# Strassen weight sums of an up projection: accumulating transfers in place of GpSimd additions

## What is computed

```python
def swiglu(h, w1, w3, w2):
    return (jax.nn.silu(h @ w1) * (h @ w3)) @ w2
...
yp = yp + swiglu(rmsnorm(yp, norm_ffn_g[l]), ffn_w1[l], ffn_w3[l], ffn_w2[l])
```

## Time and profile before

| | us |
|---|---|
| median of three runs | 1737.89 |
| the profiled execution: span from its first to its last instruction | 1735.7 |
| its own time, the median taken for it: 2.2 us lie around the span | 1737.9 |
| TensorE busy | 1702.0 |
| VectorE busy | 1058.7 |
| ScalarE busy | 683.9 |
| GpSimd busy | 370.5 |
| feed-forward part, layer 0 | 465 to 865 |
| feed-forward part, layer 1 | 1306 to 1735.7 |

### The profile page before, as it was taken

One profiled execution on the slowest core, in us unless ns is written; L12 is line 12 of the kernel. 1 busy time (PEld: TensorE's weight loads), 2 busy tenths in 40 slices (PEclk: granted clock), 3 DMA queues, 4 the chain that ended last, 5 costly groups with the idle time before them and its releaser, 6 DMA issues.

```text
span 1735.7 us, 27688 instructions
## 1 busy us (share of the span) xinstructions
PE 1702.0 (98%) x11360; PEld 1543.0 (89%) x11360; DVE 1058.7 (61%) x1717; ACT 683.9 (39%) x1219; POOL 370.5 (21%) x289
## 2 busy tenths in 40 slices
PE   7999998999999999999999999999999999999999
PEld 6566556797999999999989899789899999999999
DVE  3699867637667647465654424744676774655574
ACT  4111243435525525253552124633543453544352
POOL 3012100211104324132213132200110241414240
PEclk9999999999999999999999999999999999999999
DMA  8222330142303131403143221603320313122212
GB/s 263 101 77 103 93 107 28 49 195 98 104 27 138 32 130 46 135 19 128 31 141 74 75 73 64 246 27 114 153 93 25 128 48 115 61 70 86 87 66 91
DMA packets 39674, 162.30 MB, mean 94 GB/s; under 512 B 9384, under 2 KB 10280, under 8 KB 25600
## 3 DMA queue, kind: packets, MB, share of 16 engines
q1 hardware_dynamic: 32240, 124.59, 21.5%
q0 software_dynamic: 7312, 35.98, 5.8%
HBM read 149.87 MB, written 10.42 MB: 92 GB/s over the span
## 4 chain that ended last, share of the span: by engine, by line
PE 92%; DVE 5%; ACT 2%; issue 1%; DMA 0%; POOL 0%; SPq 0%; DVEq 0%; ACTq 0%
PE G L940 68%; PE S L940 11%; PE Q L940 11%; PE Q L1635 1%; ACT work L1731 0%; DVE rstd L2344 0%; DMA ring<-in_w_mk 0%; DVE ev_low L2593 0%; ACT rstd L1731 0%; DVE stats L2623 0%; DVE resid L2875 0%; ACT h_split L1731 0%; PE Q L1347 0%; DVE stats L2992 0%; DVE work L2636 0%
## 5 line engine op out<-in xcount | busy, mean ns | idle before, releaser
L940 PE MATMUL G<-ffn_rows,w_split 128*128 128x320 f32 x2160 | 329.8, 309 | 0.0
L940 PEld LDWEIGHTS G<-ffn_rows,w_split 128*128 128x128 f32 x2160 | 320.1, 188 | 0.0
L1731 ACT ACTIVATE w_split<-ring 128x512 fp32r<-128x512 f32 (+2 forms) x224 | 159.1, 711 | 316.8 <-PE G L940 208.4
L940 PE MATMUL G<-front,ring 128*128 128x128 f32 (+2 forms) x832 | 223.3, 430 | 11.0 <-DMA ring<-in_w_mk 9.3
L940 PEld LDWEIGHTS G<-front,ring 128*128 128x128 f32 x832 | 133.0, 193 | 100.0 <-issue 95.9
L856 POOL TENSOR_TENSOR mkT<-ring 128x512 f32<-128x512 f32 x72 | 98.2, 1369 | 564.6 <-DMA ring<-in_w_up 382.2
L940 PE MATMUL G<-h_split,w_split 128*128 128x320 f32 x1344 | 200.9, 310 | 1.2 <-DVE w_split L2359 0.8
L940 PEld LDWEIGHTS G<-h_split,w_split 128*128 128x128 f32 x1344 | 197.5, 188 | 1.9 <-issue 1.3
L940 PE MATMUL G<-g_split,w_split 128*128 128x320 f32 x1056 | 163.7, 310 | 0.1
L940 PEld LDWEIGHTS G<-g_split,w_split 128*128 128x128 f32 x1056 | 156.7, 188 | 1.7 <-DVE w_split L2848 1.4
L2715 DVE TENSOR_TENSOR w_split<-ring,w_split 128x512 fp32r<-128x512 f32 (+1 forms) x124 | 105.8, 854 | 59.9 <-ACT w_split L1731 58.7
(11 more groups left out here) (351 smaller groups left out, 2818.8 us busy)
## 6 DMA issues: line engine op xcount, KB each, us to landing
ring<-in_w_up SPq DMA_DIRECT2D x44, 1024.0 KB, 4.8
ring<-in_w_down SPq DMA_DIRECT2D x48, 256.0 KB, 2.6
ring<-in_w_down SPq DMA_DIRECT2D x32, 320.0 KB, 2.9
front<-in_mem_k POOLq DMA_DIRECT2D x8, 1024.0 KB, 6.1
front<-in_mem_v POOLq DMA_DIRECT2D x8, 1024.0 KB, 10.6
ring<-in_w_mk SPq DMA_DIRECT2D x4, 1024.0 KB, 5.9
ring<-in_w_mv SPq DMA_DIRECT2D x4, 1024.0 KB, 10.9
ring<-in_w_glu SPq DMA_DIRECT2D x4, 1024.0 KB, 8.6
```

The costliest lines, as they stand in the source:

```text
L940: return nc.tensor.matmul(out, lhsT, rhs, start=start, stop=stop, **kw)
L1731: return nc.scalar.activation(*a, **k)
```

## The change

The four sums are made by transfers. For each Strassen tile SP loads the first addend of each sum from DRAM into its buffer (`first_addends`, 256 KB each), and GpSimd issues four transfers that add into the buffer: sums 0 and 1 get a second block from DRAM, sums 2 and 3 get sum 0 and sum 2, out of SBUF. Each buffer has a semaphore for the load (`first_in`) and one for the accumulation (`sum_in`). A transfer adds and does not subtract, so all sums are of plus signs, and the signs move into the rows and the additions behind the products. The up weights are laid out in DRAM by block, so that each block is 512 contiguous columns.

```diff
-        UP = ((0, 0), (5, "b12-b11"), (6, "b22-b12+b11"), (1, 1), (3, "b12-b22"), (4, 3), (2, "b21-b22+b12-b11"))
+        UP = ((0, 0), (5, "b11+b12"), (6, "b11+b12+b22"), (1, 1), (3, "b12+b22"), (4, 3), (2, "b11+b12+b22+b21"))
         UP_BANK = (0, 2, 0, 1, 0, 2, 0)
-        SUMS = ("b12-b11", "b12-b22", "b22-b12+b11", "b21-b22+b12-b11")
+        SUMS = ("b11+b12", "b12+b22", "b11+b12+b22", "b11+b12+b22+b21")
+        BLOCK = 4 * P
+        SUM_FIRST = (0, 2, 3, 1)
...
+            def first_addends(l, f):
+
+                q = strassen(l, f)
+                for n, i in ((0, 2), (2, 2), (1, 4), (3, 6)):
+                    sp.wait_ge(op_low, operand(l, f - 1, i) + 1 if f > PLAIN else operand(l, 0, 1) + 1)
+                    if n == 2 and q:
+                        sp.wait_ge(sum_in[3], 16 * q)
+                    at = BLOCK * SUM_FIRST[n]
+                    sp.dma_start(wsum[n], dram[f"w_up{l}"][f, :, at:at + BLOCK]).then_inc(first_in[n], 16)
...
                 idx = CHUNKS[c][1]
+                if CHUNKS[c - RING][0][:4] == "w_up":
+                    l, f = int(CHUNKS[c - RING][0][4]), CHUNKS[c - RING][1]
+                    if f == 0:
+                        first_addends(l, PLAIN)
+                    elif PLAIN <= f < KH - 1:
+                        first_addends(l, f + 1)
                 load(c, slice(idx, idx + 1), slot_free(c))
...
-            def weight_sum(l, f, n):
-
-                b11, b21, b12, b22 = (up_block(l, f, block) for block in range(4))
-                a, b = ((b12, b11), (b12, b22), (b22, wsum[0]), (b21, wsum[2]))[n]
-                q = strassen(l, f)
-                if n == 0:
-                    chunk_wait(pool, CHUNK[f"up{l}", f])
-                if f > PLAIN:
-                    pool.wait_ge(op_low, operand(l, f - 1, (1, 4, 2, 6)[n]) + 1)
-                if n >= 2:
-                    pool.wait_ge(sum_ready, 4 * q + (1, 3)[n - 2])
-                nc.gpsimd.tensor_tensor(wsum[n], a, b, ALU.subtract).then_inc(sum_ready, 1)
+            def add_weights(l, f, n, src):
+
+                done = 16 * (strassen(l, f) + 1)
+                pool.wait_ge(first_in[n], done)
+                pool.dma_start(wsum[n], src, accum_op=ALU.add).then_inc(sum_in[n], 16)
+
+            def weight_sums(l, f):
+
+                done = 16 * (strassen(l, f) + 1)
+                b12, b22 = (dram[f"w_up{l}"][f, :, BLOCK * block:BLOCK * (block + 1)] for block in (2, 3))
+                add_weights(l, f, 0, b12)
+                pool.wait_ge(sum_in[0], done)
+                add_weights(l, f, 2, wsum[0])
+                add_weights(l, f, 1, b22)
+                pool.wait_ge(sum_in[2], done)
+                add_weights(l, f, 3, wsum[2])
...
-                    act.wait_ge(sum_ready, 4 * strassen(l, f) + SUMS.index(UP[i][1]) + 1)
+                    act.wait_ge(sum_in[SUMS.index(UP[i][1])], 16 * (strassen(l, f) + 1))
...
-                        out, a, b, op = ((raw7[:, 5, 1], raw7[:, 5, 1], raw7[:, 6, 0], ALU.add),
+                        out, a, b, op = ((raw7[:, 5, 1], raw7[:, 5, 1], raw7[:, 6, 0], ALU.subtract),
                                          (raw7[:, 6, 1], raw7[:, 5, 1], raw7[:, 4, 0], ALU.subtract),
                                          (two_rows(raw7[:, 4, 1]), row_source(1), two_rows(raw7[:, 6, 1]),
-                                          ALU.subtract))[i - KD]
+                                          ALU.add))[i - KD]
...
-                    v.tensor_tensor(row_diff_raw, raw7[:, 6, 1], raw7[:, 6, 0], ALU.subtract).then_inc(row_diff, 1)
+                    v.scalar_tensor_tensor(out=row_diff_raw, in0=raw7[:, 6, 1], scalar=-1.0, in1=raw7[:, 6, 0],
+                                           op0=ALU.mult, op1=ALU.subtract).then_inc(row_diff, 1)
...
-                    v.tensor_tensor(u3, u3, p5, ALU.add).then_inc(c22_ready, 1)
+                    v.tensor_tensor(u3, p5, u3, ALU.subtract).then_inc(c22_ready, 1)
...
-                    v.tensor_tensor(u2, z, u2, ALU.add).then_inc(c12_read, 1)
+                    v.tensor_tensor(u2, z, u2, ALU.subtract).then_inc(c12_read, 1)
...
-        arrays[f"w_up{l}"] = _weights(_paired(a["ffn_w1"][l], a["ffn_w3"][l]))
+        arrays[f"w_up{l}"] = np.concatenate([_weights(a[w][l], P) for w in ("ffn_w3", "ffn_w1")], axis=2)
```

More of the change, by code:

```diff
@@ L527, in build @@
         od_rows_hi, od_rows, od_high, od_split = map(sem, ("od_rows_hi", "od_rows", "od_high", "od_split"))
-        op_high, op_low, sum_ready, up_done = map(sem, ("op_high", "op_low", "sum_ready", "up_done"))
+        op_high, op_low, up_done = map(sem, ("op_high", "op_low", "up_done"))
+        first_in, sum_in = ([sem(f"{name}{i}") for i in range(4)] for name in ("first_in", "sum_in"))
         row_norm, row_sum, row_diff, row_high, row_low = map(
@@ L646, in up_block @@
         def up_block(l, f, block):
-            w = ring[:, CHUNK[f"up{l}", f] % RING, :].rearrange("p (k n) -> p k n", k=KD)
-            kh, nh = block % 2, 1 - block // 2
-            return w[:, 4 * kh:4 * kh + 4, nh * P:(nh + 1) * P]
+            at = BLOCK * block
+            return ring[:, CHUNK[f"up{l}", f] % RING, at:at + BLOCK].rearrange("p (k n) -> p k n", k=4)
         def up_operand(l, f, i):
             if f < PLAIN:
-                w = ring[:, CHUNK[f"up{l}", f] % RING, :].rearrange("p (k n) -> p k n", k=KD)
-                hi, lo = (ws[:, i, part, :].rearrange("p (k n) -> p k n", k=KD) for part in range(2))
-                return w[:, :, i * P:(i + 1) * P], hi, lo
+                src = ring[:, CHUNK[f"up{l}", f] % RING, (1 - i) * KD * P:(2 - i) * KD * P]
+                return src, ws[:, i, 0, :], ws[:, i, 1, :]
             name = UP[i][1]
@@ L843, in cross_weights @@
                     output_low(l, i)
-            def weight_sum(l, f, n):
-                b11, b21, b12, b22 = (up_block(l, f, block) for block in range(4))
-                a, b = ((b12, b11), (b12, b22), (b22, wsum[0]), (b21, wsum[2]))[n]
-                q = strassen(l, f)
-                if n == 0:
-                    chunk_wait(pool, CHUNK[f"up{l}", f])
-                if f > PLAIN:
-                    pool.wait_ge(op_low, operand(l, f - 1, (1, 4, 2, 6)[n]) + 1)
-                if n >= 2:
-                    pool.wait_ge(sum_ready, 4 * q + (1, 3)[n - 2])
-                nc.gpsimd.tensor_tensor(wsum[n], a, b, ALU.subtract).then_inc(sum_ready, 1)
+            def add_weights(l, f, n, src):
[11 more added lines that the diff above has]
+                add_weights(l, f, 3, wsum[2])
             def ffn_sums(l):
                 for f in range(PLAIN, KH):
-                    for n in range(4):
-                        weight_sum(l, f, n)
+                    weight_sums(l, f)
             cross_weights(0, TILE0["evout"], TILE0["evout"] + 7)
```

## The result

The changed kernel takes 1789.05 us (median of 4 runs, 1786.79 to 1790.2) against 1737.83 us: a ratio of 1.0291, with a 95% interval from 1.0277 to 1.0306. It is slower by 51 us. The likeliest case of the prediction, no change, did not come; the time lies at the upper end of the range, where the dear accumulations stood ("at 5 each 53 us, 1791").

The account below looks back on a forecast made before the run. TensorE was taken as the bound, busy 1702.0 of 1735.7 us. Removed sums, added transfers, signs and layout were each costed at 0, giving 1738 us, no change (chance 0.60), with a range from 1734 to 1790 us.

Parts of the forecast that it names:

- the dear accumulations: Rival at the wait ahead of operand 2: accumulations cost more than their bytes; 1763 to 1875 us, chance 0.29.
- The bound, and what a faster producer can win: Feed-forward stages: TensorE is busy nearly throughout, so faster weight sums have about 1 us to win.
- The place and the window: Loop from operand 2's low part through sums 0 and 2 to the next tile's operand 2: 10.99 us available.
- The price per us: Each us by which the loop outgrows the period costs 28 us, from 28 steps between tiles.
- the decision point: In the loop ahead of operand 2: the cover is gone when the two accumulations together pass 8.1 us.
- Both signs of being wrong: ScalarE waiting for sum 2 with TensorE gaps before product 2 or 3 in 28 places, or SP loads over 2.6 us.
- the sum: 2.6 + 3.7 + 2.9 + 0.3 = 9.5 us: Loop's load, accumulation from DRAM, accumulation from SBUF and four wake-ups; fits 10.99 us with 1.5 to spare, costing 0.
- dearer than their bytes: Rival at the wait ahead of operand 2: each element is read, added, written back; 1791 us at 5 each, chance 0.29.
- The held-up issue: Rival: VectorE delays GpSimd's writing out of transfers, making the loop 11.1 us; 1747 us, chance 0.07.
- The turn through sums 2 and 3: Sum 2's first addend waits for the last sum 3: 8.4 us a turn, under 12.32.
- SP does stand for sum 3: SP's load queue: if SP waited for sum 3, the load would go out late, with a whole tile in hand; costed 0.
- GpSimd's busy time: Sign in the changed profile: GpSimd's busy time falls by some 215 us, all of it sums.

Follow-up runs that it names:

- e5: The changed kernel with its signs, weight order and row sums kept, but the four sums as GpSimd additions again and no transfers added: 1738.07 us.
- e6: The changed kernel with two buffers each for sums 0 and 2, their first addends let go a tile earlier, GpSimd's order changed, all transfers kept: 1740.71 us.
- e3: The changed kernel without the loads and accumulations of sums 1 and 3 and the waits for them: 1744.71 us.
- e4: The changed kernel with sum 0's second transfer a plain copy that does not add, all else kept: 1772.27 us.
- e1: The changed kernel with sum 0's buffer released by operand 1's low part and the accumulation into sum 2, no longer by operand 2's low part: 1756.34 us.
- e2: The changed kernel with a second buffer for sum 0, so its first addend can be loaded a tile earlier, all transfers kept: 1759.27 us.

## Why the prediction was partly right

**The bound, and what a faster producer can win: right.** GpSimd's contention with VectorE is gone: the gate's low part takes 826 ns in the median and 827 at most, where it took up to 1920; in e5, with the additions back on GpSimd, it takes up to 1919 again.

```profile
L2798 DVE TENSOR_TENSOR g_split<-work,g_split x44: 817/826/827, 477.6 to 1755.5; 128x640 fp32r<-128x640 f32 x44
```

The Trainium skill, in "SBUF — State Buffer", section "Who interferes with whom", says that a VectorE instruction with two SBUF inputs contends with a GpSimd instruction that reads SBUF. The trace agrees (827 ns at most without such instructions, up to 1920 with them). The relief was worth nothing, since TensorE did not wait for VectorE: e6 has it and is not faster than the kernel before.

**The place and the window: right. The price per us: right for the steps inside a pass.** The loop is the one named, it has 28 steps, and the decision point was 8.1 us for two accumulations. In the turn above they take 4.82 + 3.71 = 8.5 us, load and wake-ups 0.8 us more than priced. Both signs of being wrong came: the gap before product 2 in 26 of the "28 places", and loads on SP that land later than 2.6 us. What the price of 28 us for each us left out are the longer first steps of the passes of five tiles and the slower matmuls behind them.

**The step that failed is the sum: 2.6 + 3.7 + 2.9 + 0.3 = 9.5 us.** It was 3.12 + 4.82 + 3.71 + 0.6 = 12.3 us against the window of 10.99. The wake-up of GpSimd from a transfer is 0.28 us, not the 0.1 read from waits for other engines. But the larger part is that each link was priced by a row of a lone transfer, while the change itself raised the engines' share from 0.09 to 0.83. The prediction cited the 0.09 to cost SP's loads at nothing, and did not add up the eight transfers. The lone prices were good: 3.7 us from DRAM as taken, 3.3 from SBUF against 2.9. With them and the wake-ups as measured, 2.6 + 3.7 + 3.3 + 0.6 = 10.2 us, the loop would have fitted; in e3, with half of the traffic gone, it does fit, at 10.7 us.

**The rival "dearer than their bytes" came true in place, and only partly for its reason.** An accumulation is dearer than a copy (e4) and holds the engines twice as long as a plain load (26.1 against 12.7 us of engine time); yet with half of the traffic it fits (e3), and what broke the window was the traffic of all eight transfers. That its 1791 us lie 2 us from the measured time is partly luck: they stand for 5 us for each accumulation, 10 us for the two, which take 8.5; the longer load, the wake-ups, the first steps of the passes of five tiles and the slower matmuls make up the rest.

**The held-up issue: not seen** (e4); an issue takes 0.86 us instead of 0.55, but evenly. **The turn through sums 2 and 3, priced at 8.4 us: mis-sized in the same way.** It takes over at 13.2 to 13.8 us as soon as the first loop is opened (e1, e2). SP does stand for sum 3, 26 times:

```profile
SPq L718 <- DMA mv<-mv: 59.1, 26, 3.0
```

In the changed kernel that wait is not the end of the chain, as costed; in e1 and e2 it is. **GpSimd's busy time** fell by 91 us (370.5 to 279.8), not by 215: the page counts the accumulating issues, 0.86 us and more each, as busy.

## What to carry to other kernels

Price a chain of transfers with the traffic that the change itself adds: first sum the engine time per turn, and where the share comes near 0.8, as here, take landing times from a stretch as busy as that, not from lone ones. Then look at which waits close into a loop, price every such loop and not only the first, and compare each with the period of the bound engine. Opening one of two loops of like length brought back some six tenths of the loss here (e1, e2), opening both nearly all (e6).

## What was not expected of the hardware

Accumulating transfers take 0.86 us to issue from GpSimd where a plain one takes 0.57 (e4), and hold the DMA engines about twice as long as a plain load of the same size.

After three of the four gaps in the first steps of the passes of five tiles TensorE ran slower: windows of the changed kernel (us, TensorE busy, granted clock, DMA share, GB/s), TensorE's timeline in them, and last the gap that had no such effect.

```profile
1532.00:1536.00 4.00, 2.87 (x11) 0.56 0.70 184
1536.00:1540.00 4.00, 4.00 (x19) 0.59 0.70 156
...
1533.13 8.29 PE L960 MATMUL G<-ffn_rows,w_split 128*128 128x320 f32 x36 [3.88 <-ACT work L1751]
...
1428.47 5.51 PE L960 MATMUL G<-ffn_rows,w_split 128*128 128x320 f32 x36 [3.69 <-ACT work L1751]
```

It had stood idle for 3.88 us; then the granted clock was 0.56 and 0.59 of 2.4 GHz, mostly the lower level of 1.2 GHz, and 36 matmuls took 8.29 us instead of 5.44. Behind the gaps of 1.99 and 3.42 us (at 563 and 669 us) 36 matmuls took 7.0 us, with stretches at 0.50. Behind the fourth, of 3.69 us, the clock stayed at 1.00, so the length of the gap alone does not tell whether the clock falls. The turn shown at the top, with 1.07 us of TensorE idle in its 13.57, has 1.00. A late sum can thus cost more than its own lateness; the three places cost some 6 us of this execution.
